# TensorE's expert loop with two blocks per turn and the first block ahead of it

## The reference

```
logits = h @ router_w + router_b                 # h: 1024 tokens x 1024
top_v, top_i = top_k(logits, 4)                  # 4 of 32 experts per token
# assignments sorted by expert into blocks that hold rows of one expert only
def expert_block(xblk, e):
    gu   = xblk @ w_gu[e] + b_gu[e]              # 1024 -> 2048
    gate = min(gu[:, ::2], 7);  up = clip(gu[:, 1::2], -7, 7)
    act  = (up + 1) * gate * sigmoid(1.702 * gate)
    return act @ w_down[e] + b_down[e]           # 1024 -> 1024
y[tok] += gate_weight * expert_block(...)
```

## Time and profile before

| | |
|---|---|
| median of 3 runs | 2677.33 us (2676.52 to 2683.94) |
| the profiled execution | 2674.82 us |
| its span, first to last instruction | 2673.0 us |
| granted TensorE clock, mean | 0.970 of full |
| PE busy | 2431.1 us, 91% |
| DVE, ACT, POOL busy | 1805.6, 1556.7, 808.7 us |
| moved by DMA | 536.91 MB |

### The profile page before, as it was taken

One profiled execution on the slowest core, in us unless ns is written; L12 is line 12 of the kernel. 1 busy time (PEld: TensorE's weight loads), 2 busy tenths in 40 slices (PEclk: granted clock), 3 DMA queues, 4 the chain that ended last, 5 costly groups with the idle time before them and its releaser, 6 DMA issues. The chain is left out here.

```text
span 2673.0 us, 135770 instructions
## 1 busy us (share of the span) xinstructions
PE 2431.1 (91%) x57165; PEld 2153.8 (81%) x57165; DVE 1805.6 (68%) x2119; ACT 1556.7 (58%) x1972; POOL 808.7 (30%) x638
## 2 busy tenths in 40 slices
PE   6999998999988759999899989988889999999993
PEld 2455558999984449989898989988888999999993
DVE  3786986666657772552818377777877686788883
ACT  4524544555555352553737467777776676677873
POOL 3222116767731121221212232222222222223230
PEclk9999998999999869999999999999999999999996
DMA  8621001101122283572919397889988797899965
GB/s 286 242 77 62 1 16 35 31 24 31 31 91 80 95 331 95 170 258 56 372 33 371 121 337 261 309 315 345 334 300 315 283 321 253 285 330 369 330 244 195
DMA packets 123432, 536.91 MB, mean 201 GB/s; under 512 B 12236, under 2 KB 12608, under 8 KB 90560
## 3 DMA queue, kind: packets, MB, share of 16 engines
q1 hardware_dynamic: 107120, 481.80, 48.2%
q0 software_dynamic: 14880, 48.91, 8.2%
q10 hardware_dynamic: 1360, 5.24, 0.5%
HBM read 496.99 MB, written 38.92 MB: 200 GB/s over the span
## 5 line engine op out<-in xcount | busy, mean ns | idle before, releaser
L2523 PE MATMUL ps<-qkv,weights 128*128 128x64 f16 x10496 | 938.2, 193 | 68.0 <-DVE weights L1937 34.1
L2523 PEld LDWEIGHTS ps<-qkv,weights 128*128 128x128 f16 x10496 | 922.0, 98 | 85.4 <-DVE weights L1937 40.0
L2525 PE MATMUL ps<-qkv,weights 128*128 128x64 f16 x10496 | 937.8, 193 | 4.9 <-issue 4.9
L2524 PE MATMUL ps<-qkv,weights 128*128 128x64 f16 x10496 | 937.8, 193 | 0.1
L2525 PEld LDWEIGHTS ps<-qkv,weights 128*128 128x128 f16 x10496 | 922.5, 98 | 2.4 <-issue 2.4
L2524 PEld LDWEIGHTS ps<-qkv,weights 128*128 128x128 f16 x10496 | 922.5, 98 | 0.2 <-issue 0.2
L1937 DVE SCALAR_TENSOR_TENSOR weights<-hT,weights 128x2048 f16<-128x2048 f16 (+1 forms) x256 | 587.8, 2346 | 167.4 <-ACT weights L1320 138.1
L1320 ACT ACTIVATE weights<-hT 128x2048 f16 (+1 forms) x256 | 527.1, 2101 | 87.1 <-DMA hT<-in_w_gu_dram 65.4
L2540 PE MATMUL ps<-qkv,weights 128*128 128x64 f16 x5248 | 472.8, 193 | 24.6 <-DVE weights L1942 22.3
L2540 PEld LDWEIGHTS ps<-qkv,weights 128*128 128x128 f16 x5248 | 461.7, 98 | 32.3 <-DVE weights L1942 27.9
L2541 PE MATMUL ps<-qkv,weights 128*128 128x64 f16 x5248 | 472.5, 193 | 0.0
(11 more groups left out here) (450 smaller groups left out, 4308.2 us busy)
## 6 DMA issues: line engine op xcount, KB each, us to landing
hT<-in_w_gu_dram SPq DMA_DIRECT2D x256, 1024.0 KB, 8.6
qkv<-in_w_down_dram SPq DMA_DIRECT2D x128, 1024.0 KB, 6.2
weights<-in_w_ada_dram SPq DMA_DIRECT2D x8, 2048.0 KB, 14.4
qkv<-in_w_in_dram SPq DMA_DIRECT2D x4, 2048.0 KB, 9.0
qkv<-in_w_ada_dram SPq DMA_DIRECT2D x4, 2048.0 KB, 8.7
hT<-decay_rows SPq DMA_DIRECT2D x20, 256.0 KB, 3.3
hT<-beta_rows SPq DMA_DIRECT2D x20, 256.0 KB, 3.3
qkv<-in_x_dram ACTq DMA_DIRECT2D x4, 1024.0 KB, 8.1
```

The lines of the kernel that those rows point to most:

```text
L2523: pe.matmul(dst, ghi[k][:, b, c], xT[:, 0, k, :], start=first, stop=False, skip_group_check=True)
L2524: pe.matmul(dst, ghi[k][:, b, c], xT[:, 1, k, :], start=False, stop=False, skip_group_check=True)
L2525: last = pe.matmul(dst, glo[k][:, b, c], xT[:, 0, k, :], start=False, stop=end, skip_group_check=True)
```

## The change

Block 0's gate_up and turn_x are written out ahead of the loop. The loop then has MAXB // 2 = 47 turns, each with the whole body written out twice, for t = 2 pair + 1 and t = 2 pair + 2, each copy under its own condition `t <= nlast`. The inner condition `t > 0` is gone. No other engine's program changes.

```diff
-            with pe.Fori(0, MAXB) as t:
-                with pe.If(t <= nlast):
-                    for k in range(GK):
-                        gate_up(t, k)
-                    turn_x(t + 1)
-                    with pe.If(t > 0):
+            for k in range(GK):
+                gate_up(0, k)
+            turn_x(1)
+            with pe.Fori(0, MAXB // 2) as pair:
+                for i in (1, 2):
+                    t = pair * 2 + i
+                    with pe.If(t <= nlast):
+                        for k in range(GK):
+                            gate_up(t, k)
+                        turn_x(t + 1)
                         turn_y(t)
                         down(t)
             turn_y(nlast + 1)
```

## The result

| | before | after |
|---|---|---|
| median, us | 2677.01 (4 runs) | 3194.09 (4 runs, 3188.64 to 3204.07) |
| profiled execution, span | 2673.0 | 3202.3 |
| granted TensorE clock | 0.970 | 0.919 |
| q8 instruction packets | 45 | 493 |

The ratio is 1.1931, with a 95% interval of 1.1911 to 1.1951. The change makes the kernel slower by a fifth of its time, 517 us.

A forecast was written before the change was run, and what follows sets the result against it. PE's own stream was taken to bound the loop. 2674.8 + 444 (running on) + 185 (branch back) + 7 (tail) - 5 (block 0's branch) - 60 (waits) - 9 (seams) = 3237, so 3239 us; range 2800 to 3430, likeliest case 2985 to 3430.

The forecast's parts named there:

- all eleven packets fetched again in each of 40 turns: PE's new loop touches 10 code packets, 11 with the one ahead; all refetched every turn, some 440 more; chance 0.52.
- the branch back, less today's seams: End of each PE loop turn: 40 fetch waits, 4.85 us on average, less the 0.23 there now; +185 us.
- running on, 2.9 us in each packet with new weights: Within the 32 blocks with new weights: each of 4.8 packets takes 6.8 us instead of 3.9; +444 us.
- the waits for DVE's weights and sums: PE's 34.1 + 22.3 + 7.6 us of waits for DVE: a slower PE mostly finds them done; -60 us.
- the seams between the copies: Between the two copies of a turn: the 41 gaps of 0.23 us go; -9 us.
- the tail: Empty turns behind PE's loop: 3 fetches of 3.6 us and 16 branches of 0.37, 17 us for 9.5; +7.
- block 0's branch: Block 0's branch over turn_y and down, with 5.32 us of "issue" before block 1, goes; -5 us.
- The capacity: How much loop code PE keeps: 6 packets shown kept, 11 needed; the case that all is fetched again got 0.52.
- only part is fetched: Rival for PE's loop code: with fixed places, say eight, 6 of 11 packets come per turn; about 2980 us; chance 0.26.
- the whole loop stays: Rival: PE holds all 11 packets, 176 KB; 2660 to 2667 us, or unchanged at 2670 to 2677; chance 0.14.
- The fetch: Cost per code packet on PE: 6.8 us with DMA full, from block 0's two stops; 3.6 quiet, from the gathers.
- the ends of the terms: Limits of the sum: 2987 us with 5.3 us fetches; 3411 with clock recoveries (+120) and the worse tail (52 more).

The follow-up runs named there:

- peel_one_copy: Against the changed kernel: block 0 still ahead of the loop, but one copy of the body per turn; ratio 1.0011 to the kernel before.
- quiet_pair: The changed kernel with only the first expert's weights loaded and halved, all blocks computed with them, so DMA stays quiet; 2807.93 us.
- dead_copy: Against peel_one_copy: a second copy behind the one that runs, in the same loop, under a condition that never holds; 3032.05 us (1.1403).

## Why the prediction was right

It said 3239 us, likeliest in 2985 to 3430, and 3194 came; slower was given 0.86. The terms against what they measured in the profiled execution, in us:

| step of the prediction | predicted | measured |
|---|---|---|
| all eleven packets fetched again in each of 40 turns | 440 more on q8 | 448, of them 8 for the longer program |
| the branch back, less today's seams | +185 | 175.6 - 9 = +166 |
| running on, 2.9 us in each packet with new weights | +444 | stops within blocks about +300, half clock about +123 |
| the waits for DVE's weights and sums | -60 | about -64, none left |
| the seams between the copies | -9 | about -1: 8.2 us are left |
| the tail | +7: 17 for 9.5 | +8: 17.4 for 9.5 |
| block 0's branch | -5 | block 1 starts 5.4 us earlier; no gain in peel_one_copy (1.0011) |

The 300 are the 273 us of idleness within the blocks and about 0.16 us for each of some 170 stops, in which the last matmul before the stop counts as busy. The 123 come as in quiet_pair from the mean durations: 200 ns for L2523 instead of 193, 14% of 31488 matmuls at 24 ns more are 108 us, and 195 for L2540, 4% of 15744, are 15. (Counted one by one, 5143 of the loop's matmuls start at the half clock, 24 ns more each, again 123.) Together the terms give 166 + 300 + 123 + 8 - 64 - 1 - 5 = 527; 10 us of smaller waits of the kernel before are gone too, which leaves 517 of the 529 us between the two spans. The other 12 are not accounted for.

**The capacity** was the step with the widest choice: the rows showed six packets kept and nothing of eleven, and the case in which all of them are lost got 0.52. It was right: 8 packets held, 11 needed, none of them kept. The rivals that only part is fetched, or that the whole loop stays, are out by the count of packets, and they fall a second time at 9 and 10.

**The fetch.** The two stops of block 0 were read rightly: one packet ahead, slower than its code only when DMA is full. The quiet fetch that was worked out from the gathers (3.6 us) was met by 3.60.

**The mis-sized term** is running on. "With DMA quiet only the branch back costs, with DMA full everything does", 2.9 us a packet, would be 444; the stops came to about 300. And the clock, which stood only among the ends of the terms ("in full stretches that costs little"), cost 123. The price of a packet was too high: counted between the places of the stops, the code of a packet passed in 6.0 us on average where DMA was at 0.9 or more and the clock full (74 packets), and in 6.4 where the clock had fallen for part of it (23), not in the 6.8 read from block 0. That the sum of the two, 423, still lies near 444 is in part luck. About two thirds of the half-clock matmuls started where DMA was at 0.9 or more, where a slower PE has less to wait for. The rest came where it was less busy, and for those the prediction had nothing in its sum; in quiet_pair, where nearly all the stops within the blocks are gone, the clock costs 77 us by itself.

**The seams between the copies** were misread, at a size that doesn't matter: the prediction let all 9 us go, and looked for no stop there, but the second copies still begin after 0.2 us each, 8.2 in all. So that pause is not the branch back's own. What it is isn't shown.

**The tail** came out within 1 us, 17.4 for 17. q8 brings five packets there in three goes (3140.9 and 3141.2, 3146.4 and 3146.6, 3151.3), and three waits of 3.6 us and 16 branches of 0.37 are 16.7. After that the empty turns keep their few packets, although they jump over code they don't run; dead_copy shows the same in most of its turns.

**The waits for weights** went wholly, as forecast, but a reader of the wait table alone would think that they only changed their shape (32.6 us for 34.1). Their count and longest gave it away.

## What to carry to other kernels

Before writing more copies of a body into a hardware loop on PE, count its instructions, a weight load and a matmul for each product: at 256 per packet, the packets that the loop touches and one more must not be over eight (128 KB). A jump within the loop adds to the count, since the packet ahead of the place it leaves may be asked for too: dead_copy comes to nine that way and lost 14%. How many packets a loop touches depends on where it begins: the one copy of dead_copy is 4.8 packets long and touches six. At eight or fewer, without such a jump, a copy is free and gains next to nothing (a seam was 0.23 us in 18.75); one over, and the whole loop is fetched in each turn. In the changed kernel that cost 3.4 to 6.3 us at each branch back, in quiet_pair 3.6 on average, and with DMA full more within the turn. The queue of instruction packets on the page tells it at a glance: during a loop it must stand still.

## What the runs showed that I had not expected

- A stop of 3.6 us at a branch back, in a loop in which PE was hardly ever idle otherwise, was enough to take the clock to its lower level until some 5 us after it (1295 to 1301 in the windows above), in 39 of the 40 turns: 77 us on top of the 144 in quiet_pair.
- A hint at the very head of the loop, a whole turn ahead of the branch, took the stops at the branch back from 175.6 us to 60.5, and about 91 us off the time.
- In dead_copy code that never runs cost 14%: the set of packets was lost in 22 of 80 turns, mostly after turns in which nothing had been fetched. The set is nine by the places of the stops; what tells the turns apart is open.
